# Attention of a streaming encoder step: both heads of a pair go block by block

## What is computed

```
p = x @ w_in                                 # A q,k,v | B q,k,v | gate A | gate B
yA = band attention, 16 heads of 64, own chunk of 64 + 8 previous, bias per head
yB = sliding attention, 16 query heads on 2 k/v heads, own chunk + 2 previous, sinks
per head:  s = q k^T / 8 + bias;  m = max(s)  (mixer B: max(m, sink))
           pr = exp(s - m) / sum;  o = pr @ v
h = LayerNorm(alpha x + (sigmoid(gA) yA Wa + sigmoid(gB) yB Wb) Wout)
y = LayerNorm(alpha h + PEER(h))             # product keys, 16384 experts
```

## Time and profile before

| what | value |
|---|---|
| median of the runs | 4470.74 us |
| span of the profiled execution | 4456.8 us (its own time outside the span isn't listed; the median is 13.9 us above it) |
| PE busy over the span | 4282.4 us, 96% |
| attention stage | 515.4 to 1312.5 us, 797.1 us |
| PE busy in it | 391.79 of 397.6 us and 387.25 of 399.5 us |
| a pair | about 52 us for mixer A, 47 to 49 us for B |

### The profile page before, as it was taken

How to read it: one execution, slowest core, us unless ns; L and a number is a source line. 1 busy time by engine, 2 the same in 40 slices (tenths; PEclk the granted TensorE clock), 3 DMA queues, 4 the chain that set the end, 5 groups by cost and what they waited for, 6 DMA issues and landing times.

```text
span 4456.8 us, 71381 instructions
## 1 busy us (share of the span) xinstructions
PE 4282.4 (96%) x26508; PEld 4120.7 (92%) x26508; DVE 2839.1 (64%) x4233; ACT 1376.0 (31%) x2750; POOL 2672.1 (60%) x1665
## 2 busy tenths in 40 slices
PE   8999999999989999799899999999999999999998
PEld 8999888878879999699899999999999999999997
DVE  1000133444442231699997899898997988988988
ACT  1000122222221110311386434343443443443444
POOL 5444322222324545244776778778887888888884
PEclk9999999999999999999999999999999999999999
DMA  5222233222233323112489999999999999999995
GB/s 202 99 102 98 96 119 128 104 81 81 78 119 122 116 90 99 38 66 76 145 276 320 382 376 398 374 372 409 416 405 377 412 418 411 417 411 416 418 418 241
DMA packets 269138, 1083.82 MB, mean 243 GB/s; under 512 B 24560, under 2 KB 90224, under 8 KB 185328
## 3 DMA queue, kind: packets, MB, share of 16 engines
q0 software_dynamic: 74736, 544.24, 29.8%
q1 hardware_dynamic: 89568, 391.16, 23.6%
q10 hardware_dynamic: 104736, 147.39, 9.7%
HBM read 1020.44 MB, written 67.63 MB: 244 GB/s over the span
## 4 chain that ended last, share of the span: by engine, by line
PE 66%; DVE 18%; DMA 6%; issue 5%; POOL 3%; ACT 1%; ACTq 0%; DVEq 0%; POOLq 0%
PE banks L497 30%; PE banks L741 15%; PE banks L675 11%; DVE work L1499 3%; DVE work L1462 2%; DVE banks L1465 2%; POOL w_lo L383 2%; PE banks L729 2%; DMA work<-in_u_rows,idx_all 2%; PE banks L566 2%; PE banks L528 2%; DMA work<-in_v_rows,idx_all 1%; POOL work L411 1%; PE banks L536 1%; DVE work L1371 1%
## 5 line engine op out<-in xcount | busy, mean ns | idle before, releaser
L383 POOL TENSOR_TENSOR w_lo<-w_raw,w_hi 128x1024 fp32r<-128x1024 f32 x472 | 1140.7, 2417 | 243.5 <-ACT w_hi L1057 229.6
L389 POOL TENSOR_SCALAR w_hi<-w_raw 128x2048 fp32r<-128x2048 f32 x134 | 289.6, 2161 | 1326.8 <-PE banks L497 1252.3
L497 PE MATMUL banks<-mv_hi,w_hi 128*128 128x256 f32 x3648 | 863.2, 318 | 62.9 <-DVE mv_lo L1203 35.4
L497 PE MATMUL banks<-mv_lo,w_hi 128*128 128x256 f32 x3648 | 835.8, 310 | 0.0
L497 PE MATMUL banks<-mv_hi,w_lo 128*128 128x256 f32 x3648 | 835.3, 310 | 0.0
L497 PEld LDWEIGHTS banks<-mv_hi,w_hi 128*128 128x128 f32 x3648 | 652.1, 189 | 127.1 <-issue 85.9
L741 PE MATMUL banks<-mv_hi,w_hi 128*128 128x384 f32 x2048 | 693.2, 338 | 43.5 <-ACT part_t L1116 22.1
L393 POOL TENSOR_TENSOR w_lo<-w_raw,w_hi 128x512 fp32r<-128x512 f32 x536 | 721.0, 1377 | 11.2
L675 PE MATMUL banks<-mv_hi,w_hi 128*128 128x384 f32 x2048 | 694.0, 339 | 4.6 <-ACTq L1083 2.0
L741 PE MATMUL banks<-mv_lo,w_hi 128*128 128x384 f32 x2048 | 690.3, 337 | 0.0
L741 PE MATMUL banks<-mv_hi,w_lo 128*128 128x384 f32 x2048 | 690.3, 337 | 0.0
(11 more groups left out here) (166 smaller groups left out, 5319.5 us busy)
## 6 DMA issues: line engine op xcount, KB each, us to landing
w_raw<-in_wstream SPq DMA_DIRECT2D x472, 512.0 KB, 7.9
w_raw<-in_wstream SPq DMA_DIRECT2D x134, 1024.0 KB, 4.8
gate_matrix<-work ACTq DMA_DIRECT2D x12, 2048.0 KB, 9.0
work<-gate_matrix ACTq DMA_DIRECT2D x32, 768.0 KB, 9.0
out_p<-work ACTq DMA_DIRECT2D x34, 320.0 KB, 2.2
work<-out_p ACTq DMA_DIRECT2D x34, 320.0 KB, 3.4
gate_scratch<-work ACTq DMA_DIRECT2D x32, 320.0 KB, 2.2
work<-gate_scratch ACTq DMA_DIRECT2D x16, 640.0 KB, 4.0
```

What stands on the lines that cost most here:

```text
L383: pool.tensor_tensor(w_lo[s][:, part], raw[s][:, part], w_hi[s][:, part].bitcast(f32), ALU.subtract) \
L389: pool.tensor_scalar(w_hi[s][:, :], raw[s][:, :], 1.0, 0.0, ALU.mult, ALU.add).then_inc(hi_done, 1)
L497: last = pe.matmul(acc(dst, h), a[s][:, P * k:P * k + P], b[h][:, k, :], start=(k == k_first and n == 0), stop=(k == k_last and n == 2))
```

## The change

The pair's items are listed block by block, both heads of a block next to each other, and every engine's loop goes over the blocks u (`NU` = 5) with two items in each turn. PE does the scores of both heads, then k_steps, the two transposes with k_steps between them, and then the values of block u-2, whose products alternate between the heads. The buffers `s_sb` and `pt_sb` become four; the score banks stay two, the transpose bank one. The number of products is the same.

```diff
-        HEADS = [(hh, i) for hh in range(2) for i in range(4)] + [(0, "sample"), (1, "sample")]
+        HEADS = [(hh, i) for i in (0, 1, 2, 3, "sample") for hh in range(2)]
+        NU = NS // 2
...
-            def scores(mix, j, t):
+            def scores(mix, j, u):
+                i = HEADS[2 * u][1]
+                if u:
+                    pe.wait_ge(s_taken, 1 + STEP_BASE[mix] + NS * j + 2 * u)
...
+                for lo, hi in pieces:
+                    for hh in range(2):
+                        rows = slice(HD * hh, HD * hh + HD)
...
+                        last = pe.matmul(s_bank[hh][:, at + lo:at + hi], q_t[rows, span], k_t[rows, first + lo:first + hi],
+                                         start=True, stop=True)
...
-            def values(mix, j, t):
+            def values(mix, j, u):
...
                     for c in range(nk):
                         kb = i + 2 - nk + c
-                        last = pe.matmul(o, v_nat[:, P * kb + HD * hh:P * kb + HD * hh + HD], pt[:, P * c:P * c + P],
-                                         start=(c == 0), stop=(c == nk - 1))
-                last.then_inc(o_full, 1)
+                        for o, at, pt in parts:
+                            last = pe.matmul(o, v_nat[:, P * kb + at:P * kb + at + HD], pt[:, P * c:P * c + P],
+                                             start=(c == 0), stop=(c == nk - 1))
+                            if c == nk - 1:
+                                last.then_inc(o_full, 1)
...
-                for t in range(NS + 2):
-                    if t < NS:
-                        scores(mix, j, t)
-                    before = {0: 0, 1: 1, 6: 1, 7: 1} if mix == "a" else {0: 1, 6: 1, 7: 1, NS: 3}
-                    gemm(before.get(t, 2))
-                    if 1 <= t <= NS:
-                        transpose_p(mix, j, t - 1)
-                    if t >= 2:
-                        values(mix, j, t - 2)
-                    if t == 6:
-                        gemm(2)
+                for u in range(NU + 2):
+                    if u < NU:
+                        scores(mix, j, u)
+                    spread = ((1, 0, 0), (2, 1, 1), (1, 1, 1), (1, 1, 1), (1, 1, 1), (2, 1, 0), (2, 0, 0)) if mix == "a" else \
+                        ((2, 0, 0), (2, 1, 1), (1, 1, 1), (1, 1, 1), (2, 1, 1), (2, 1, 1), (2, 0, 0))
+                    early, between, late = spread[u]
+                    gemm(early)
+                    if 1 <= u <= NU:
+                        transpose_p(mix, j, 2 * u - 2)
+                        gemm(between)
+                        transpose_p(mix, j, 2 * u - 1)
+                        gemm(late)
+                    if u >= 2:
+                        values(mix, j, u - 2)
+                    if u == 3:
                         cached_scores(mix, j)
+                gemm(len(k_steps))
...
-                    for t in range(NS + 2):
-                        if 1 <= t <= NS:
-                            soft_out(mix, j, t - 1)
-                        if t < NS:
-                            soft_in(mix, j, t)
-                        if t >= 2:
-                            out_take(mix, j, t - 2, j + (PAIRS if mix == "b" else 0))
+                    for u in range(NU + 2):
+                        for t in (2 * u, 2 * u + 1):
+                            if u < NU:
+                                soft_in(mix, j, t)
+                        for t in (2 * u - 2, 2 * u - 1):
+                            if 1 <= u <= NU:
+                                soft_out(mix, j, t)
+                        for t in (2 * u - 4, 2 * u - 3):
+                            if u >= 2:
+                                out_take(mix, j, t, j + (PAIRS if mix == "b" else 0))
```

More of the change, by code:

```diff
@@ L512, in _ @@
                     unit(s, U_QKV + 2 * i + s, (qkv_evac, 2 * i + s + 1), 0)
-            def scores(mix, j, t):
[L516 to L520, removed]
+            def scores(mix, j, u):
+                i = HEADS[2 * u][1]
+                if u:
+                    pe.wait_ge(s_taken, 1 + STEP_BASE[mix] + NS * j + 2 * u)
+                else:
+                    pe.wait_ge(s_taken, 1 + STEP_BASE[mix] + NS * j)
                 if i == "sample":
                     pe.wait_ge(t_taken, 1 + t_use(mix, j, ("c", 0), 1))
-                    pe.transpose(bank[:, 0:P], st_sb[hh][:, :], ident)
-                    last = pe.matmul(bank[:, P:2 * P], q_t[rows, 0:P], k_t[rows, 0:P], start=True, stop=True)
-                else:
[L526 to L529, removed]
+                    for hh in range(2):
+                        pe.transpose(s_bank[hh][:, 0:P], st_sb[hh][:, :], ident)
+                    at, span, pieces = P, slice(0, P), ((0, P),)
+                else:
+                    w, end = width(mix, i), P * (i + 2)
+                    at, span = 0, slice(end - P, end)
+                    pieces = ((0, w),)
+                for lo, hi in pieces:
+                    for hh in range(2):
+                        rows = slice(HD * hh, HD * hh + HD)
+                        first = span.stop - pieces[-1][1] if i != "sample" else 0
+                        last = pe.matmul(s_bank[hh][:, at + lo:at + hi], q_t[rows, span], k_t[rows, first + lo:first + hi],
+                                         start=True, stop=True)
+                        if hi == pieces[-1][1]:
+                            last.then_inc(s_full, 1)
             def transpose_p(mix, j, t):
@@ L535, in transpose_p @@
                 for c in range(w // P):
-                    last = pe.transpose(t_bank[:, P * c:P * c + P], s_sb[t % 2][:, P * c:P * c + P], ident)
+                    last = pe.transpose(t_bank[:, P * c:P * c + P], s_sb[t % 4][:, P * c:P * c + P], ident)
                 last.then_inc(t_full, 1)
@@ L546, in cached_scores @@
                 last.then_inc(t_full, 1)
-            def values(mix, j, t):
[L549 to L553, removed]
+            def values(mix, j, u):
+                i = HEADS[2 * u][1]
+                pe.wait_ge(t_taken, 1 + t_use(mix, j, ("t", 2 * u + 1), 1))
+                pe.wait_ge(o_taken, 1 + STEP_BASE[mix] + NS * j + 2 * u)
+                v_nat = vn if mix == "a" else vn_b
+                parts = [(o_bank[HD * hh:HD * hh + HD, 0:P], HD * hh, pt_sb[(2 * u + hh) % 4]) for hh in range(2)]
                 if i == "sample":
@@ L557, in values @@
                         c = DEC_T * b
[L558 to L561, removed]
+                        for o, at, pt in parts:
+                            pe.matmul(o[:, c:c + DEC_T], cv_t[:, P * b + at:P * b + at + HD],
+                                      pt[:, c:c + DEC_T], start=(b == 0), stop=False)
+                    for o, at, pt in parts:
+                        pe.matmul(o, v_nat[:, at:at + HD], pt[:, P:2 * P], start=False, stop=True).then_inc(o_full, 1)
                 else:
@@ L1243, in soft_out @@
                 dve.wait_ge(e_ready, STEP_BASE[mix] + NS * j + t + 1)
-                total = rsum[t % 2]
+                total = rsum[t % 4]
                 if mix == "b":
-                    own.done(dve.tensor_tensor(den[t % 2], rsum[t % 2], esink[t % 2], ALU.add))
+                    own.done(dve.tensor_tensor(den[t % 2], rsum[t % 4], esink[t % 4], ALU.add))
                     own.wait()
```

62 lines of the change are left out of this document (33 added, 29 removed).

## The result

The changed kernel takes 4509.36 us (median of 4 runs, 4502.93 to 4516.39), the kernel before 4470.73 us. The ratio is 1.0086, with a 95% interval of 1.0071 to 1.0101: slower by 39 us, where 78 were forecast. The profiled execution took 4510.77 us with a span of 4509.0.

The account below looks back on a forecast made before the run. PE's instruction list was taken to bound the attention stage. Waits 114, long scaling 11 and clock 18, less 13 for old waits, 32 for passages and 20 for overlap, gave +78: 4549 us, likely 4520 to 4580, wider range 4500 to 4590.

Parts of the forecast that it names:

- The waits: Attention stage: PE waits for DVE's scaling before transposes and ACT's copy before sample scores, 114 us over 16 pairs.
- the long scaling: Scalings slowed while POOL splits weights, about one per pair that PE waits for: 11 us, bounds 0 and 22.
- The overlap of the heads: Values and scores of two heads run partly side by side on PE: 20 us gained, bounds 0 and 41.
- The clock: PE's clock falls behind the new waits above 2 us: 18 us lost, bounds 0 and 54.
- The list: PE's instruction list in the attention stage gets shorter, by 32 us for fewer passages and 20 us for overlap.
- the passages between forms: PE changes less often between scores, values, transposes and k_steps: 2.0 us saved per pair, 32 us for 16.
- Rival 1: Products in different array halves overlap fully, 41 us instead of 20, without clock loss: +39 us, 4510 us; chance 17%.
- Rival 2: The clock falls at nearly every wait above 1.5 us, 54 us instead of 18: +114, 4585 us; chance 12%.
- Rival 3: PE's waits are half as long or less; at a third, 38 us, the total is -27, 4444 us; chance 8%.

Follow-up runs that it names:

- Experiments 2 to 5: Each against the changed kernel: DVE's soft_out before soft_in, 4509.31 us; ACT's takes before exponentials, 4515.66; both swaps, 4366.57; k_steps moved ahead of the first transpose, 4422.39.
- Experiment 6: Changed kernel with two added products of unused result behind the early k_steps of turns u = 2 to 4: 4480.74 us.
- experiment 7: Changed kernel with one small full-array transpose between the scores of a block's two heads, so that they can't overlap: 4520.46 us.
- experiment 9: Changed kernel with DVE's and ACT's orders both swapped, k_steps moved ahead of the first transpose, and cached_scores ahead of block 1's values: 4392.81 us.

## Why the prediction was half right

**The waits: right in place, and nearly in size.** 116 us were measured. 114 were reckoned, and 11 for the long scaling beside them. The chain is a little shorter than reckoned (588.42 - 583.78 = 4.64 us at 512 keys, 4.80 in the prediction). Its cover is shorter still: 1.06 us of scores instead of 1.92. So that wait is 2.42 us and not 1.9. Experiments 2 to 5 show the cause, with one thing that the prediction did not see: ACT's order is a second gate right behind DVE's, and mending DVE's alone gives nothing.

**The overlap of the heads: this step failed.** The prediction bounded it at 41 us and took 20, "Each float32 product is two instructions on the same half, so at best every second neighbour can overlap". The rows after show that the whole work of one head runs beside the other's. Values: half of 544 x 0.107 us, 29 us. Sample values: 16 x 1.30 us, 21 us. Scores: the whole stream of the second head, 2.13 us for a pair of A, 1.5 for B and 0.21 for each sample, 32 us. Together 82 us, twice the stated upper bound and four times the value taken. Two errors made the bound: the sample values were taken to be at a floor, and the scores to lose half of a head and not all of it. The Trainium skill's rule, in TensorEngine Tiling (Array Packing), Key Properties, that different tiles execute weight loads and products in parallel, is what the traces agree with: 32 sample instructions take 0.95 us, where 16 took 0.96. It had been set aside as unshown and given 17%.

**The clock: right mechanism, a third of the size.** 18 us were taken, "a third" of an upper bound of 54. By the table 55 us are lost after and 4 before, which makes 51: nearly the upper bound. This second step failed in the other direction and hid more than half of the first error. Experiment 6 shows the cause: filling the waits with useless products takes the clock back up.

**The list.** It is 112 us shorter by the table (780 to 668), and 52 were forecast, 32 for the passages between forms and 20 for the overlap. By the rows it should be 32 + 82 = 114 us, so the term for the passages holds and nothing is left unexplained. Not all of it is worth its time: the scores' share stands ahead of a wait that doesn't end sooner, and in experiment 7 a list of 66 us more cost 11.

**The sum.** +102 (idle time, 120.5 against 18.1) + 51 (clock) - 112 (list) = +41, against 42 in the stage of the two profiled executions and 39 between the medians. The forecast was +112 + 18 - 52 = +78. The measured 4509 us lie just under the forecast 4520 to 4580 and inside the wider range. The spans of the two profiled executions differ by 52 us, 10 of them outside this stage. The 13.9 us by which the median of before lies above its profiled span were no fixed part outside the span: after, execution and span differ by 1.8 us. The profiled execution of before was a quick one, and where in it these us lie is open.

**The rivals.** Rival 1 (full overlap, no clock loss) gives 4510 and ends where the measurement is, but by two errors that cancel: its overlap, 41 us, is half the true one, and its clock loss is missing. Rival 2 had the clock nearly right (54 us against 51) and the time wrong. Rival 3, half the waits, did not happen.

## What to carry to other kernels

When an edit makes a stage's main engine faster and puts a hand-over into its path, work out both from the start of the same instruction: what is saved ahead of a wait is worth little. Here an edit that put 66 us into the list ahead of the waits, 32 of them the overlap of the scores, cost 11. Before leaving such a loop, read for each wait which instruction of each other engine stands ahead of the one that releases it; two orders that each look harmless were two gates in a row, and only mending both gave 143 us. Small products that use half the rows or half the columns should stand next to one of the other half, alternating where the runs of one half are long: four instructions in a row lost nothing here, eight did. And keep the clock's loss apart from the idle time when a stage is taken apart, since PE is busy, only slower, in most of the time at 1.2 GHz.

## What the runs showed of the hardware

- Float32 products on different halves of the array overlap fully, in rows (scores: 1.06 us for two heads, 1.05 for one) and in columns (values: 8 in 0.58 us, against 6 in 0.80), weight loads included (sample values: 32 in 0.95 us, against 16 in 0.96).
- It works without alternation: four instructions of one half and then four of the other take 0.59 us. Eight and eight take 1.51 us, against 1.02 alternating. A full-array product between them ends it: 2.37 us for two heads' scores instead of 1.06.
- In the stage of the changed kernel PE waits 67 times for the scaling, 1.6 us on average and 3.2 at most. The mean clock there is 0.92: 136.5 us at 1.2 GHz, PE busy in 122 of them. Two instructions of a k_step take 0.53 us there and 0.30 at 2.4 GHz. Products that compute nothing, put into these idle times, brought the mean to 0.98 and made the program 28.6 us faster.
- Idle times needn't be long for that. In mixer B of experiment 9 none is over 1.2 us, but three of them (0.77, 1.19 and 0.47 us) stand so close that PE is busy for 2.10 of 4.5 us, and the 10 us behind run at 1.2 GHz.
